# Serving six gathered rows ahead of tile 64, none in the last six tiles, and spreading the products that add up set 0

## The chip, the cores and the metric

The kernel runs on one NeuronCore of a Trainium2 chip. The metric is device time in microseconds of one execution. The engines work at once and meet at semaphores: TensorE (PE, with its weight loads as PEld), VectorE (DVE), ScalarE (ACT), GpSimd (POOL) and SyncE (SP). POOL and SP also issue transfers: SP the plain ones, POOL the indirect ones (gathers by index), and one set of 16 DMA engines carries both.

## The reference, cut to what matters

The model has two layers. Each ends in a feed-forward stage in which every one of 256 tokens picks 16 experts for each of 8 heads out of 16384:

```
u = jnp.take(expert_u, idx, axis=0)
act = gelu(einsum('chkd,cd->chk', u, xc))
vsel = jnp.take(expert_v, idx, axis=0)
return einsum('chk,chkd->cd', gate * act, vsel)
x = x + peer_ffn(rms_norm(x, norm_ffn[l]), ...)
```

An expert is one row of 2048 numbers of `peer_u` and one of `peer_v`. The change lies in this stage alone.

## The kernel before, in words

The stage is the function `experts`, called once in each layer. It treats the 256 tokens in two ways.

160 tokens (`DENSE`) are done densely on PE. **Sweep 1** runs over 128 tiles of `peer_u`; a tile is 128 experts, 1 MB, 16 products of 128x160 (L1753). SP streams the tiles into a ring of four (`ex_tile`). ACT takes each result through the GELU (L1870, L1872). From tile 64 (`FIRST`) to tile 103, each tile is preceded by a product of one-hot matrices that spreads the gates of four tokens over the experts (L1762); ACT copies it (L1909), DVE multiplies it in (L2083) and builds the next one-hot matrices (L1999, L2000). DVE also multiplies each tile's GELU by its gates (L2086). **Sweep 2** runs over 128 tiles of `peer_v` (L1826), which POOL gathers (L1703), by index lists `ex_wanted` that DVE makes eight tiles at a time (`want`, L2012 to L2014: 13 of the 16 pieces in tiles 104 to 116, the last three after the loop over the tiles).

The other 96 tokens come in three sets of 32. A set has 32 picks in each of four partition quarters, so a *row step* gathers one expert row for each of 128 partitions: 32 steps in `peer_u` (a dot product on DVE, L2028), then 32 in `peer_v` (a weighted sum on DVE, L2031 and L2034). That makes 192 steps, numbered n = 0 to 191. Steps 0 to 31 are the dots of set 0, 32 to 63 its sums, 64 to 95 the dots of set 1, and so on. POOL gathers them, 1 MB each, into a ring of three (`ex_row`): the gather of step n waits until step n-3 is served. `served(j)` says how many steps DVE has done by the end of sweep 1's tile j: 30 before tile 64, then one with each tile, 94 at the end. `rows_ahead` derives from it how many gathers POOL issues before sweep 2's first tile (92), each as two half rows (L1692); after that five gathers of whole rows (L1686) are put between every six gathers of `peer_v` tiles, all in one queue, in order. Step 32 needs `weigh(0)` on ACT (L1895), which takes the dots of set 0 through the GELU; the same holds for the other sets.

When a set is summed, four small products (`fold`, L1789) add its quarters up and DVE adds each into `x` (`fold_add`, L2043). They use two PSUM banks in turn, so the third product of a set waits for the first addition. Set 0 is folded in front of tiles 114 to 117 (`FOLD_0`), set 1 in front of tiles 64, 66, 68 and 70 of sweep 2, with DVE's additions in front of steps 147, 149, 151 and 153. `widen` (L1776) spreads a set's tokens over the partitions before its dots.

In front of tile 62 PE transposes the picks (L1801), for which DVE must have made the shares (`share(0)`, L1971 to L1973), for which ACT must have taken the exponentials (`exps(0)`, L1877, in front of tile 60). ACT copies the transposed picks (L1904), and DVE can build one-hot matrices.

Two more waits matter. PE's tile j waits until ACT has taken tile j-3 (three banks). From tile 66 on ACT's GELU of tile j goes into one of two buffers and waits until DVE has multiplied tile j-2.

Each engine runs its own program in the order written, and a wait holds all that stands behind it on that engine, its transfers too.

Of the kernel before, what the change touches and what calls it, by code (L numbers as in the profile page):

```python
# [8 lines left out]
P = 128  # L9
# [7 lines left out]
TB = SEQ // P  # L17
# [13 lines left out]
PEER_H, KEYS, TOPK = 8, 128, 16  # L31
# [5 lines left out]
SET, SETS, STEPS = 32, 3, 32  # L37
# [2 lines left out]
GROUP = 4  # L40
GROUPS = DENSE // GROUP
FIRST = 64
BEFORE = 30
WIDEN_0, EXPS_1, WIDEN_1, FOLD_0 = 2, 16, 90, 114
WIDEN_2, FOLD_1, FOLD_1_AT = 28, 64, 147
A_BANKS = (4, 5, 3)
G_BANKS = (0, 1, 2)
# [1539 lines left out]

def served(j):

    return BEFORE + max(j - FIRST + 1, 0)  # L1590


def experts(nc, t, layer, sem, sb, bank, c, x, hT, query, W, low, layer_base, row_in, v_in, cols, cols_in):
# [22 lines left out]
    with ExitStack() as st:  # L1616
# [19 lines left out]
        share_w = sb(st, "ex_share", [P, SETS, STEPS])  # L1636
        dot, dot_gelu = sb(st, "ex_dot", [P, STEPS]), sb(st, "ex_dot_gelu", [P, STEPS])
        weight = sb(st, "ex_weight", [P, STEPS])

        over = lambda name, shape, kb, dt=F32: nc.alloc_sbuf_tensor_at(name, shape, dt, offset=int(scratch + kb * 1024))  # L1640
        left, cand = over("ex_left", [P, 256], 0), over("ex_cand", [P, TOPK, TOPK], 1)
# [5 lines left out]
        pos = over("ex_pos", [P, TOPK], 5.375, U32)  # L1647
        half_u = over("ex_half_u", [P, 2, TOPK], 5.5, U32)
        half_f = over("ex_half_f", [P, 2, TOPK], 5.625)
        total = over("ex_total", [P, TB, 2, PEER_H], 5.75)  # L1650
        picks = nc.alloc_sbuf_tensor_at("ex_picks", [P, TB, 3, PEER_H, TOPK], F32, offset=before_hot)
        best = nc.alloc_sbuf_tensor_at("ex_best", [P, TB, PEER_H, TOPK], F32, offset=before_hot + 3072)
        outT = W[:, 0:KT, :]
# [3 lines left out]
        with nc.Block() as block:  # L1657
# [59 lines left out]
            def _(pe):  # L1717
# [61 lines left out]
                def fold(s, n):  # L1779

                    pe.wait_ge(sums_ready, s + 1)
                    r = slice(SET * (s + 1), SET * (s + 2))
                    if n >= 2:
                        pe.wait_ge(fold_added, 4 * s + n - 1)
                    elif s < 2:
                        pe.wait_ge(wide_out, (7, 11)[s] + n)
                    else:
                        pe.wait_ge(fold_added, 7 + n)
                    mmul(bank[r, 6 + n % 2, :], c("fold"), sums[:, n * GW:n * GW + GW], start=True, stop=True)\  # L1789
                        .then_inc(fold_mm, 1)  # L1790

                for j in range(TILES):
                    if 0 <= j - WIDEN_0 < 4:
                        widen(0, j - WIDEN_0)
                    if j == FIRST - 2:
                        pe.wait_ge(picks_ready, TB)
                        pe.wait_ge(wide_out, 3)
                        for i in range(3):
                            for b in range(TB):
                                n = min(P, DENSE - b * P)  # L1800
                                mm = tr(bank[:, 6, i * DENSE + b * P:i * DENSE + b * P + n],  # L1801
                                        picks[0:n, b, i].rearrange("p h k -> p (h k)"), c("ident")[0:n, 0:n])
                        mm.then_inc(picks_mm, 1)
                    if 0 <= j - FIRST < GROUPS:
                        gates(j - FIRST)
                    if 0 <= j - WIDEN_1 < 4:
                        widen(1, j - WIDEN_1)
                    if 0 <= j - FOLD_0 < 4:
                        fold(0, j - FOLD_0)
                    tile(j)  # L1810

                pe.wait_ge(gates_times, GROUPS)
# [34 lines left out]
            def _(act):  # L1847
# [49 lines left out]
                for j in range(TILES):  # L1897
                    if j == EXPS_1:
                        exps(1)
                    if j == FIRST - 4:  # L1900
                        exps(0)
                    if j == FIRST - 2:
                        act.wait_ge(picks_mm, 1)
                        A.copy(picksT[:].rearrange("p a s -> p (a s)"), bank[:, 6, 0:3 * DENSE]).then_inc(picks_out, 1)  # L1904
                    g = j - FIRST
                    if 0 <= g < GROUPS:
                        act.wait_ge(gates_mm, g + 1)
                        src = bank[:, G_BANKS[g % len(G_BANKS)], :].rearrange("p (c e) -> p e c", c=GROUP)
                        A.copy(W[:, j:TILES, GROUP * g:GROUP * g + GROUP], src[:, j:TILES, :]).then_inc(gates_put, 1)  # L1909
                    for s, first in enumerate((WIDEN_0, WIDEN_1)):  # L1910
                        if j == first - 1:
                            if s == 0:
                                act.wait_ge(h_scaled, 4)
                            four_times(s, 0)
                        if 0 <= j - first < 4:
                            widened(s, j - first)
                    tile(j)
                    if served(j - 1) < STEPS <= served(j):
                        weigh(0)
                weigh(1)  # L1920
                four_times(2, 0)
                for g in range(4):
# [2 lines left out]
                for i in range(6):  # L1925
                    act.wait_ge(out_mm, i + 1)
                    n = min(3, KT - 3 * i)
# [4 lines left out]
            def _(dve):  # L1932
# [130 lines left out]
                    for n in range(2 * h, 2 * h + 2):  # L2063
                        serve(n)
                over_best(0)
                for n in range(2 * PEER_H, served(FIRST - 1)):
                    serve(n)
                share(0)

                dve.wait_ge(picks_out, 1)  # L2070
                one_hot(0)
                one_hot(1)

                for j in range(FIRST, TILES):
                    g = j - FIRST
                    if 0 <= j - FOLD_0 < 4:
                        fold_add(0, j - FOLD_0)
                    if g < GROUPS:
                        dve.wait_ge(gates_put, g + 1)
                        dve.wait_ge(tile_out, j)  # L2080
# [69 lines left out]
```

## Time and profile before

| | |
|---|---|
| Time before, median of 3 runs | 3850.46 us (3844.37 to 3850.97) |
| The profiled execution | 3844.62 us, span 3842.8 us |
| PE busy | 3703.6 us (96%) |
| DVE busy | 2355.8 us (61%) |
| POOL busy | 1222.3 us (32%) |
| L1753, products of sweep 1 | 8192, 1133.9 us |
| L1826, products of sweep 2 | 8192, 1116.7 us |
| L2028, dots of gathered rows | 192, mean 2292 ns |
| L2034, sums of gathered rows | 186, mean 2350 ns |

Busy time is a share of the span. The span runs from the first to the last instruction. Times in a timeline count from its start. Sweep 1 of layer 1 begins at 2648.83 us, sweep 2 at 3262.55 us; in layer 0 they begin at 733.92 us and 1348.59 us.

### The profile page before, as it was taken

Reading aid. Unit: us, or ns where it says so; the run is one execution under the profiler, and the core shown is the slowest. Engines: PE = TensorE matmul, PEld = TensorE weight load, DVE = VectorE, ACT = ScalarE, POOL = GpSimd, SP = SyncE. Lnnn points to the kernel's source line nnn. Section 1 sums busy time; section 2 is a strip of 40 time slices with the busy share of each in tenths; the row PEclk is TensorE's granted clock in tenths of the full one; section 3 lists DMA queues with packets and bytes.
Section 4 is the critical chain, followed back from the end, with each engine's and each line's share of the span. In section 5 each row is a group of like instructions: output and inputs, shape, how many; then the busy total and the mean of one; then the engine's idle time right before and its main releaser. Section 6 shows DMA issues by size and latency. Waiting matters only on the chain. (4 is left out here: it accounts for less than half of the span.)

```text
span 3842.8 us, 63592 instructions
## 1 busy us (share of the span) xinstructions
PE 3703.6 (96%) x26848; PEld 3413.9 (89%) x26848; DVE 2355.8 (61%) x4207; ACT 429.8 (11%) x1020; POOL 1222.3 (32%) x936
## 2 busy tenths in 40 slices
PE   7998999999999999999979989999999999999998
PEld 6776895899999899999967868959999998999998
DVE  5975853884488754444369658538944986544442
ACT  1013220100111000000010132211101110000000
POOL 2610000033133365655335110000331334555553
PEclk9998999999999999999989989999999999999999
DMA  5441013499899999999644311135998999999996
GB/s 163 132 131 32 29 39 128 168 389 406 327 401 398 378 367 363 366 352 369 246 137 137 121 32 34 57 105 187 400 406 321 402 398 387 377 367 361 352 367 218
DMA packets 312250, 994.19 MB, mean 259 GB/s; under 512 B 59309, under 2 KB 170285, under 8 KB 230509
## 3 DMA queue, kind: packets, MB, share of 16 engines
q0 software_dynamic: 118656, 587.71, 39.5%
q1 hardware_dynamic: 193312, 402.41, 28.8%
q8 instruction: 214, 3.51, 0.4%
q14 instruction: 68, 0.56, 0.0%
HBM read 1071.38 MB, written 2.10 MB: 279 GB/s over the span
## 5 line engine op out<-in xcount | busy, mean ns | idle before, releaser
L1753 PE MATMUL bank<-ycT,ex_tile 128*128 128x160 f32 x8192 | 1133.9, 300 | 0.0
L1753 PEld LDWEIGHTS bank<-ycT,ex_tile 128*128 128x128 f32 x8192 | 1119.2, 190 | 8.7 <-issue 8.4
L1826 PEld LDWEIGHTS bank<-ex_W,ex_tile 128*128 128x128 f32 x8192 | 1113.3, 190 | 8.0 <-issue 6.7
L1826 PE MATMUL bank<-ex_W,ex_tile 128*128 128x160 f32 x8192 | 1116.7, 299 | 1.1 <-DMA ex_tile<-in_peer_v,ex_wanted 1.1
L2028 DVE CUSTOM_DVE_ANT_0 ex_row<-ex_row,ex_h_wide 128x2048 f32<-128x2048 f32 x192 | 439.1, 2292 | 389.1 <-DMA ex_row<-in_peer_u,ex_rows 386.8
L2034 DVE SCALAR_TENSOR_TENSOR ex_sums<-ex_row,ex_weight,ex_sums 128x2048 f32<-128x2048 f32 x186 | 437.1, 2350 | 364.1 <-DMA ex_row<-in_peer_v,ex_rows 364.1
L1692 POOL DMA_INDIRECT ex_row<-in_peer_u,ex_rows x240 | 259.0, 1079 | 1205.1 <-DVE ex_rows L1986 759.5
L1703 POOL DMA_INDIRECT ex_tile<-in_peer_v,ex_wanted x256 | 338.2, 1321 | 428.0 <-PE bank L1826 397.6
L335 PE MATMUL pj_bank<-pj_hT,pj_piece 128*128 128x256 f32 x2048 | 458.0, 383 | 2.5 <-DVE pj_hT L606 2.5
L335 PEld LDWEIGHTS pj_bank<-pj_hT,pj_piece 128*128 128x128 f32 x2048 | 387.4, 191 | 68.3 <-issue 13.8
L1692 POOL DMA_INDIRECT ex_row<-in_peer_v,ex_rows x128 | 121.3, 948 | 311.4 <-DVE ex_sums L2034 168.3
L1686 POOL DMA_INDIRECT ex_row<-in_peer_v,ex_rows x128 | 170.7, 1334 | 46.3 <-issue 41.4
L812 PE MATMUL bank<-arena,ycT 128*128 128x512 f32 x320 | 140.0, 593 | 2.0 <-PEq L904 2.0
L1011 PE MATMUL bank<-arena 128*128 128x128 f32 x1152 | 140.3, 280 | 0.0
L1011 PEld LDWEIGHTS bank<-arena 128*128 128x128 f32 x1152 | 136.6, 195 | 0.9
L812 PEld LDWEIGHTS bank<-arena,ycT 128*128 128x128 f32 x320 | 60.2, 190 | 75.5 <-issue 75.3
L1178 POOL TENSOR_TENSOR ycT<-ycT,rw_H 128x1024 f32<-128x1024 f32 x6 | 15.9, 2646 | 322.2 <-DVE rw_H L1349 321.8
L1467 PE MATMUL bank<-ycT,query_w 128*128 128x256 f32 x512 | 114.9, 382 | 2.0 <-PEq L1484 2.0
L1686 POOL DMA_INDIRECT ex_row<-in_peer_u,ex_rows x72 | 106.9, 1484 | 21.9 <-issue 21.9
L1872 ACT ACTIVATE ex_W<-bank 128x160 f32<-128x160 f32 (+20 forms) x206 | 56.9, 276 | 496.0 <-PE bank L1753 496.0
L1467 PEld LDWEIGHTS bank<-ycT,query_w 128*128 128x128 f32 x512 | 95.8, 190 | 16.5 <-issue 2.7
L2000 DVE TENSOR_SCALAR ex_hot<-consts,ex_picksT 128x128 f32<-128x128 f32 x320 | 110.1, 344 | 0.0
(385 smaller groups left out, 3457.6 us busy)
## 6 DMA issues: line engine op xcount, KB each, us to landing
ex_tile<-in_peer_uT SPq DMA_DIRECT2D x256, 1024.0 KB, 8.1
pj_piece<-in_w_in SPq DMA_DIRECT2D x32, 2048.0 KB, 8.7
arena<-in_w_out SPq DMA_DIRECT2D x20, 1024.0 KB, 5.1
query_w<-in_peer_w_query SPq DMA_DIRECT2D x16, 1024.0 KB, 6.1
rw_low_rank<-in_w_out SPq DMA_DIRECT2D x12, 512.0 KB, 3.5
ex_row<-in_peer_u,ex_rows POOLq DMA_INDIRECT x312, 9.7
ex_row<-in_peer_v,ex_rows POOLq DMA_INDIRECT x256, 8.9
ex_tile<-in_peer_v,ex_wanted POOLq DMA_INDIRECT x256, 8.2
```

The costliest lines, as they stand in the source:

```text
L335: mm = mmul(pj_bank[:, n % 2, m * SEQ:m * SEQ + SEQ], piece[:, n % 2, k, m * P:m * P + P], hT[:, k, :], start=(m == 0 and k == 0), stop=(k ...
L812: mm = nc.tensor.matmul(bank[:, out_bank(n) + b, :], ycT[:, br * GT + k, b * P:b * P + P], out_w["place"][:, i % PLACES, k, :], start=(br ...
L1011: mm = mmul(bank[:, b, j * P:j * P + P], left[:, d, j, :], right[:, d, j, :], start=(j == 0), stop=True, skip_group_check=True)
L1467: mm = nc.tensor.matmul(bank[:, h % 2, 0:SEQ], query["w"][:, h % WRING, k, :], hT[k // 4][:, k % 4, :], start=(k == 0), stop=(k == KT - 1) ...
L1686: nc.gpsimd.indirect_dma_start(out=place[:, n % RING, :], out_offset=None, in_=whole_rows[table][:, :], in_offset=bass.IndirectOffsetOnAxi ...
L1692: nc.gpsimd.indirect_dma_start(out=place[:, n % RING, half * D // 2:(half + 1) * D // 2], out_offset=None, in_=tables[table][:, :], in_off ...
L1703: nc.gpsimd.indirect_dma_start(out=ring[:, slot, :], out_offset=None, in_=whole_rows[1][:, :], in_offset=bass.IndirectOffsetOnAxis(ap=want ...
L1753: mm = mmul(o, ring[:, j % SLOTS, k * P:k * P + P], hT[k // 4][:, k % 4, 0:DENSE], start=(k == 0), stop=(k == KT - 1))
L1826: mm = mmul(bank[:, at_, lo:lo + DENSE], ring[:, i % SLOTS, m * P:m * P + P], W[:, j, :], start=(j == 0 and m % 3 == 0), stop=(j == TILES ...
L2000: mm = V.tensor_scalar(hot1[:, g % 2, i, :], c("iota"), picksT[:, 0, n:n + 1], picksT[:, 2, n:n + 1], ALU.is_equal, ALU.mult)
L2028: V.tensor_tensor_reduce(out=row, in0=row, in1=h_wide[:], scale=1.0, scalar=0.0, op0=ALU.mult, op1=ALU.add, accum_out=dot[:, step:step + 1 ...
L2034: V.scalar_tensor_tensor(sums[:], row, weight[:, step:step + 1], sums[:], ALU.mult, ALU.add)\
```

## The change

`served` now counts 36 steps before tile 64, then one with each tile up to 94: tiles 64 to 121 have one each, tiles 122 to 127 none. Six more steps (30 to 35) so stand on DVE between `over_best(0)` and tile 64: steps 30 and 31 ahead of `share(0)`, 32 to 34 behind it, and 35 behind the first one-hot matrices. ACT's `exps(0)` moves from tile 60 to tile 56, and `weigh(0)` stands in front of tile 59. The gathers that POOL issues ahead of sweep 2 grow from 92 to 96. `widen(1)` moves from tiles 90 to 93 to tiles 78 to 81. The folds of set 0 stand in front of tiles 112, 113, 118 and 119. `total` gets a place of its own, since the sums of set 0 now begin while it is in use.

```diff
-BEFORE = 30
-WIDEN_0, EXPS_1, WIDEN_1, FOLD_0 = 2, 16, 90, 114
+BEFORE, LAST = 36, 58
+WIDEN_0, EXPS_1, EXPS_0, WEIGH_0, WIDEN_1 = 2, 16, FIRST - 8, FIRST - 5, 78
+FOLD_0_AT = (112, 113, 118, 119)
...
-    return BEFORE + max(j - FIRST + 1, 0)
+    return BEFORE + min(max(j - FIRST + 1, 0), LAST)
...
+        total = sb(st, "ex_total", [P, TB, 2, PEER_H])
...
-        total = over("ex_total", [P, TB, 2, PEER_H], 5.75)
...
-                    if 0 <= j - FOLD_0 < 4:
-                        fold(0, j - FOLD_0)
+                    if j in FOLD_0_AT:
+                        fold(0, FOLD_0_AT.index(j))
...
-                    if j == FIRST - 4:
+                    if j == EXPS_0:
                         exps(0)
+                    if j == WEIGH_0:
+                        weigh(0)
...
-                    if served(j - 1) < STEPS <= served(j):
-                        weigh(0)
...
-                for n in range(2 * PEER_H, served(FIRST - 1)):
+                for n in range(2 * PEER_H, STEPS):
                     serve(n)
                 share(0)
-
+                for n in range(STEPS, served(FIRST - 1) - 1):
+                    serve(n)
                 dve.wait_ge(picks_out, 1)
                 one_hot(0)
                 one_hot(1)
+                serve(served(FIRST - 1) - 1)
...
-                    if 0 <= j - FOLD_0 < 4:
-                        fold_add(0, j - FOLD_0)
+                    if j in FOLD_0_AT:
+                        fold_add(0, FOLD_0_AT.index(j))
```

PE, the end of sweep 1, before (16 products of L1753 are one tile, `ex_sums` marks a fold; the first row is tiles 103 to 113):

```order
L1753 MATMUL bank<-ycT,ex_tile 128x160 x176
L1789 MATMUL bank<-ex_sums,consts 32x512
L1753 MATMUL bank<-ycT,ex_tile 128x160 x16
L1789 MATMUL bank<-ex_sums,consts 32x512
L1753 MATMUL bank<-ycT,ex_tile 128x160 x16
L1789 MATMUL bank<-ex_sums,consts 32x512
L1753 MATMUL bank<-ycT,ex_tile 128x160 x16
L1789 MATMUL bank<-ex_sums,consts 32x512
L1753 MATMUL bank<-ycT,ex_tile 128x160 x176
```

And now (every line number behind the constants is one higher):

```order
L1754 MATMUL bank<-ycT,ex_tile 128x160 x144
L1790 MATMUL bank<-ex_sums,consts 32x512
L1754 MATMUL bank<-ycT,ex_tile 128x160 x16
L1790 MATMUL bank<-ex_sums,consts 32x512
L1754 MATMUL bank<-ycT,ex_tile 128x160 x80
L1790 MATMUL bank<-ex_sums,consts 32x512
L1754 MATMUL bank<-ycT,ex_tile 128x160 x16
L1790 MATMUL bank<-ex_sums,consts 32x512
L1754 MATMUL bank<-ycT,ex_tile 128x160 x144
```

The folds start two tiles sooner, and between the second and the third now lie five tiles where there was one.

POOL's queue around the start of sweep 2, before (`ex_row` rows are gathers of steps, `ex_tile` rows those of `peer_v` tiles; x56 is 28 steps in halves, 64 to 91):

```order
L1692 DMA ex_row<-in_peer_u,ex_rows 128x1024 x56
L1703 DMA ex_tile<-in_peer_v,ex_wanted 128x2048 x2
L1686 DMA ex_row<-in_peer_u,ex_rows 128x2048
L1703 DMA ex_tile<-in_peer_v,ex_wanted 128x2048
L1686 DMA ex_row<-in_peer_u,ex_rows 128x2048
L1703 DMA ex_tile<-in_peer_v,ex_wanted 128x2048
L1686 DMA ex_row<-in_peer_u,ex_rows 128x2048
```

And now:

```order
L1693 DMA ex_row<-in_peer_u,ex_rows 128x1024 x64
L1704 DMA ex_tile<-in_peer_v,ex_wanted 128x2048 x2
L1687 DMA ex_row<-in_peer_v,ex_rows 128x2048
L1704 DMA ex_tile<-in_peer_v,ex_wanted 128x2048
L1687 DMA ex_row<-in_peer_v,ex_rows 128x2048
L1704 DMA ex_tile<-in_peer_v,ex_wanted 128x2048
L1687 DMA ex_row<-in_peer_v,ex_rows 128x2048
```

Behind the first two tiles of sweep 2 the queue held step 92, and behind each of the next ones 93 and 94; now it holds 96, 97 and 98 there, four steps further on, and so all through sweep 2.

DVE, the gap in front of tile 64, now (`ex_total` marks `share(0)`, `ex_sums` steps 32 to 34 of set 0; before, the one-hot matrices, L1999 there, stood right behind the third row). The first one-hot row is the last shown:

```order
L1972 TENSOR_REDUCE ex_total<-ex_picks 128x8
L1973 RECIPROCAL ex_total<-ex_total 128x8
L1974 TENSOR_TENSOR ex_picks<-ex_picks,ex_total 128x128
L2024 TENSOR_TENSOR ex_weight<-ex_dot_gelu,ex_share 128x32
L2032 TENSOR_SCALAR ex_sums<-ex_row,ex_weight 128x2048
L2027 REGISTER_ALU
L2035 SCALAR_TENSOR_TENSOR ex_sums<-ex_row,ex_weight,ex_sums 128x2048 x2
L2000 TENSOR_SCALAR ex_hot<-consts,ex_picksT 128x128
```

Three sum steps came in between the shares and the one-hot matrices; the step behind those is not shown.

## Rows read from the trace of the kernel before

**Rows 1.** Chain of waits, layer 1: start, us, engine, line, count.

```profile
2672.51 247.76 PE bank L1753 x1824
...
2935.55 0.89 PE bank L1762 x8
2936.45 4.35 PE bank L1753 x32
...
3131.22 0.30 ACT ex_gelu L1870
```

**Rows 2.** PE timeline, layer 1, end of sweep 1: start, us, idle before and releaser.

```profile
3137.15 47.98 PE L1753 MATMUL bank<-ycT,ex_tile 128*128 128x160 f32 x352
3185.06 1.05 PE L1789 MATMUL bank<-ex_sums,consts 128*32 128x512 f32 x2
...
3191.55 4.61 PE L1753 MATMUL bank<-ycT,ex_tile 128*128 128x160 f32 x32
3205.53 1.88 PE L1789 MATMUL bank<-ex_sums,consts 128*32 128x512 f32 x2 [9.36 <-DVE x L2043]
3207.34 6.22 PE L1753 MATMUL bank<-ycT,ex_tile 128*128 128x160 f32 x32
...
3214.47 48.08 PE L1753 MATMUL bank<-ycT,ex_tile 128*128 128x160 f32 x352
```

**Rows 3.** PE timeline, layer 0: the same fold, and the start of sweep 2.

```profile
1290.34 1.89 PE L1789 MATMUL bank<-ex_sums,consts 128*32 128x512 f32 x2 [9.01 <-DVE x L2043]
...
1348.59 122.02 PE L1826 MATMUL bank<-ex_W,ex_tile 128*128 128x160 f32 x896 [1.07 <-DMA ex_tile<-in_peer_v,ex_wanted]
```

**Rows 4.** DVE timeline, layer 1, tiles 104 to 127 of sweep 1 and after.

```profile
3147.36 2.29 DVE L2028 CUSTOM_DVE_ANT_0 ex_row<-ex_row,ex_h_wide 128x2048 f32<-128x2048 f32 x1 [0.65 <-DMA ex_row<-in_peer_u,ex_rows]
...
3192.03 2.29 DVE L2028 CUSTOM_DVE_ANT_0 ex_row<-ex_row,ex_h_wide 128x2048 f32<-128x2048 f32 x1 [2.58 <-DMA ex_row<-in_peer_u,ex_rows]
...
3196.06 0.32 DVE L2086 TENSOR_TENSOR ex_W<-ex_W,ex_gelu 128x160 f32<-128x160 f32 x1
3196.31 2.29 DVE L2028 CUSTOM_DVE_ANT_0 ex_row<-ex_row,ex_h_wide 128x2048 f32<-128x2048 f32 x1
...
3204.70 0.68 DVE L2043 TENSOR_TENSOR x<-bank,x 32x512 f32<-32x512 f32 x1
3205.41 0.33 DVE L2086 TENSOR_TENSOR ex_W<-ex_W,ex_gelu 128x160 f32<-128x160 f32 x1
...
3256.24 2.29 DVE L2028 CUSTOM_DVE_ANT_0 ex_row<-ex_row,ex_h_wide 128x2048 f32<-128x2048 f32 x1
3258.46 0.08 DVE L2028 DVE_READ_ACCUMULATOR2_ANT ex_dot<- 128x1 f32 x1
...
3272.81 1.48 DVE L2012 TENSOR_REDUCE ex_hot<-ex_W 128x8 f32<-128x1280 f32 x1
...
3278.22 2.29 DVE L2028 CUSTOM_DVE_ANT_0 ex_row<-ex_row,ex_h_wide 128x2048 f32<-128x2048 f32 x1
```

**Rows 5.** Windows: stretch, its length, busy PE, PEld, DVE, ACT, POOL; clock, DMA, GB/s.

```profile
2888.00:2921.00 33.00, 33.00 (x243) 32.60 (x241) 0.78 (x3) 5.31 (x11) 1.86 (x2) 1.00 0.83 319
...
3000.00:3060.00 60.00, 60.00 (x460) 60.00 (x459) 54.81 (x128) 7.42 (x33) 21.64 (x24) 1.00 1.02 401
...
3137.00:3185.00 48.00, 48.00 (x355) 47.88 (x354) 32.22 (x46) 3.28 (x11) 18.00 (x18) 1.00 1.02 414
3185.00:3207.00 22.00, 12.64 (x71) 9.20 (x70) 18.97 (x26) 0.91 (x3) 7.51 (x8) 0.85 1.01 404
```

**Rows 6.** DVE timeline, layer 1, the gap in front of tile 64.

```profile
2885.41 2.29 DVE L2028 CUSTOM_DVE_ANT_0 ex_row<-ex_row,ex_h_wide 128x2048 f32<-128x2048 f32 x1 [2.76 <-DMA ex_row<-in_peer_u,ex_rows]
...
2913.58 0.29 DVE L1971 TENSOR_REDUCE ex_total<-ex_picks 128x8 f32<-128x128 f32 x1 [25.86 <-ACT ex_picks L1877]
...
2922.12 0.29 DVE L1999 TENSOR_SCALAR ex_hot<-consts,ex_picksT 128x128 f32<-128x128 f32 x1 [7.70 <-ACT ex_picksT L1904]
```

**Rows 7.** POOL timeline, layer 1: a half-row gather.

```profile
2889.22 0.94 POOL L1692 DMA_INDIRECT ex_row<-in_peer_v,ex_rows  x1 [0.30 <-issue]
```

**Rows 8.** Tile `ex_tile`, its gathers at 3786:3825 and at 3250:3300.

```profile
DMA to landing us min/median/max: 5.0/5.2/6.5
...
DMA to landing us min/median/max: 7.7/8.7/10.0
```

**Rows 9.** Timelines of PE and DVE, layer 1: first fold of set 1 and its addition.

```profile
3542.42 1.04 PE L1789 MATMUL bank<-ex_sums,consts 128*32 128x512 f32 x2
...
3550.05 0.69 DVE L2043 TENSOR_TENSOR x<-bank,x 32x512 f32<-32x512 f32 x1
```

## The prediction

> **What bounds the kernel now.** I read the chain of waits first, layer 1's feed-forward stage. It is PE almost throughout: sweep 1 runs at 247.76 / 57 = 4.35 us a tile, and at 4.35 + 0.89 = 5.24 us with a gate product [rows 1]. So only places where PE waits, or would now wait, can move the time. The PE timeline then shows one wait in sweep 1: the third fold of set 0 stands 9.36 us (9.01 in layer 0) for DVE's addition of the first [rows 2, 3]. Behind it the engine runs slow: this fold takes 1.88 us where the first took 1.05, and the next tile 6.22 where the one before took 4.61, and in that stretch the granted clock is 0.85, partly at 1.2 GHz [rows 2, 5]. That is 9.36 + 0.83 + 1.61 = 11.8 us, and the second way to count agrees: tiles 104 to 127 free of waits would take 24 x 4.35 + 4 x 0.97 = 108.3 us from 3141.5 (3137.15 + 4.35, tile 103 being the first of the eleven) to 3249.8, and sweep 1 ends at 3214.47 + 48.08 = 3262.55, 12.7 us later.
>
> DVE is late because its rows are. From the step of tile 104 at 3147.36 to that of tile 111 at 3192.03, seven steps take 44.67 us, 6.38 each, all ended by a DMA wait [rows 4], while PE goes at 4.35 and the DMA engines are full at 414 GB/s [rows 5]. The tile stream takes 1.05 MB per 4.35 us = 241 GB/s, and 1.05 MB / (414 - 241) is 6.1 us: rows get what tiles leave.
>
> **The change, part by part.** Worked in layer 1, taken twice.
>
> *The gap.* DVE idles 25.86 us ahead of `share(0)` and 7.70 us behind it, and the DMA engines run at 319 GB/s there [rows 5, 6]. Steps 30 and 31 were already on their way; at one row per 6.4 us they end near 2900. `share(0)` then waits for an exponential four tiles (17.4 us) earlier than 2913.5, and is done near 2901 instead of 2914. Step 32 waits for `weigh(0)` in front of tile 59, near 2908; steps 32 to 34 end near 2919, with row 34 landing last. DVE has to be free at 2922.1 for the one-hot matrices [rows 6]; they take 3.6 us, step 35 ends near 2928, and the gates of tile 64 are multiplied at 2931.7. So the six steps fit with about 3 us to spare, and I cost them at 0. If rows 33 and 34 come later than I think, the price is one row, 6.4 us, less the 3 of slack and the 2.8 that the one-hot matrices can slip: 0 to about 1 us.
>
> *Tiles 64 to 103.* Same steps per tile, 5.24 us a tile and 2.1 MB in it, 401 GB/s used [rows 1, 5]. The ring of rows is full at tile 64 as before. 0. `widen(1)` only moves.
>
> *The folds.* The third now stands at tile 118 and needs the addition of tile 112. DVE reaches tile 112 at 3196.06 [rows 4], PE reaches tile 118 near 3205. The wait goes, 12.7 us with its clock.
>
> *What is late next.* PE's tile j+5 waits for ACT's tile j+2, which waits for DVE's multiplication of tile j: 0.33 + 0.30 us [rows 1, 4] and small change, so tile j+5 cannot start before T(j) + 0.7. Now DVE: T(112) = 3196.06 + 0.7 for its addition (3204.70 to 3205.41) = 3196.8. Row, `want` piece and multiplication take about 4.3 us when the row is there, one more 0.85 with an addition; the ring holds the row of tile 112 at 3196.31, the next land each 6.3 us. That gives T(113) = 3202.2, T(114) = 3206.8, T(115) = 3213.1, T(116) = 3219.5. PE unheld starts tile 121 at 3141.5 + 17 x 4.35 + 3.9 = 3219.4, and DVE allows 3220.2. From here DVE's rows hold PE. Six more rows follow (tiles 116 to 121). Held, PE takes tiles no faster than rows come, so both share: 2.1 MB at 401 GB/s is 5.2 us. T(122) = 3219.5 + 31.2 = 3250.7, tile 127 starts at 3251.4, and sweep 1 ends at 3255.8: 6.8 us gained. When the last `peer_u` tile is in, rows come faster: before, the two at 3256.24 and 3258.77 stand 2.5 us apart [rows 4]. So I take 3254.1, a gain of 8.5. The ends: 12.7 if rows keep up, 0 if they stay at 6.38 a step to the end (T(122) = 3257.8, end 3262.9).
>
> *The start of sweep 2.* POOL's queue is in order. Gather 97 stands ahead of `peer_v` tile 3 and waits for step 94. Step 94 lies behind the loop over tiles and three `want` pieces: with E the start of sweep 2, ACT's GELU (0.30) and the multiplication (0.33) of tile 127 end near E + 0.95, three pieces (3272.81 to 3278.22, 5.41) bring E + 6.4, the step takes 2.3 more, and gather 97 goes at E + 8.9, tile 3 at E + 10.1 (0.94 + 0.30) [rows 4, 7]. Before, the gather at this place was step 93, whose condition (step 90) was met before E. A tile lands 5.2 us after its issue when alone, 8.7 under load [rows 8]; with one row ahead of it I take 6, E + 16.1. PE wants it at E + 13.05. Stall 3.0 us; ends 2.1 (5.0) and 5.8 (8.7) with 1.6 to 2.4 more if the clock falls. The trace has an idle of 1.07 us at this place in layer 0 after which 28 tiles take 122 us, so no fall [rows 3], and one of 9.36 with a fall; 3 us lies between, nearer the first: 0.
>
> The Trainium skill (DMA: Bandwidth & Descriptors, "Anatomy of one DMA — SWDGE (gpsimd) path") puts a transfer at 2.0 us fixed plus its bytes at 436 GB/s, by which 1.05 MB lands in an estimated 4.4 us, under the 5.0 us of the fastest tile here. By that figure the stall would be 1.5 us and the total 3 us better; the trace's landing is longer and decides.
>
> *The middle of sweep 2.* All steps run four further on, 4.8 tiles or 21 us earlier. The first fold of set 1 ended at 3543.4 and DVE came to its addition at 3550.05 [rows 9]; now DVE is there 14 us early and waits. Gather 150, which needs step 147 (3543.4 + 0.7 + 2.3, then 0.3), goes at about 3547 and holds `peer_v` tile 66, issued at 3548.2. PE wants tile 66 at 3553.3. With 6 us to land: 3554.2, stall 0.9; ends 0 and 3.6. The later additions find slack of two tiles and more.
>
> *The end of sweep 2* waits for no step. 0.
>
> Sum per layer: -8.5 + 3.0 + 0.9 = -4.6; both -9.2. The profiled execution's own 3844.62 becomes 3835.4. The median shown is 5.8 above it, and two of three runs lie there, so for the median I say 3850.46 - 9.2 = 3841.3.
>
> **The rivals.** All against the median.
>
> *Full gain:* rows keep up, because rows saved from the gap's idle transfers leave the ring fuller and the lag of 15 us at tile 112 stops growing. -2 x (12.7 - 3.9) = -17.6, and -25.4 if the waits in sweep 2 do not bite either: 3825 to 3833. For it: the allowance is nearly five tiles, and only six tiles come after it is used up. Against: 6.38 us a row over seven rows, with no sign of recovery while PE runs.
>
> *No net change, the transfers bound it:* rows stay near 6.3 a step until sweep 1 ends, the tail gains 0 to 3, the two new waits cost 3.9: 2 x (3.9 - 1.5) = +4.8, 3855. For it: 414 GB/s in that stretch is the highest in the windows. The bytes that PE and DVE need are the same.
>
> *Slower, POOL's queue:* the wait in front of `peer_v` tile 3 is the loaded one, 5.8 us, and the clock falls behind it, 2.4 more, and tile 66 costs 3.6: 11.8 a layer against the 8.5. Then +6.6 in all with the tail as forecast and +10 with a tail of 6.8: 3857 to 3861. It decides from the point where a gather behind the row lands in over 7.5 us. For it: 8.7 is the median under load. Against: at E + 8.9 nothing else is in flight.
>
> *The gap holds PE:* a late row 34 puts the one-hot matrices behind PE at tile 64 in both layers. The change then doesn't do what it says at no cost: some +3 each on top of the forecast, 3847, or worse.
>
> **How the numbers follow.** Forecast 0.45 (own range 3833 to 3847), full gain 0.22, no net change 0.14, slower queue 0.13, gap 0.06. A measurement of this kernel can tell 0.2%, 7.7 us, from no change. Faster by more: the full gain 0.22 and some 0.6 of the forecast's 0.45: 0.50. Slower by more: 0.11 of the queue, 0.03 of the others: 0.14. The same: 0.36. The range, with under 2 in 10 left out, is 3826 to 3857.
>
> **What would show it.** The idle in front of the third fold gone, PE held in its place by ACT's GELU in front of tiles 121 to 127, with T(112) near E(112) + 15; DVE's additions at tiles 112 and 113. In the gap no PE idle, `share(0)` near 2901. At sweep 2's tile 3 an idle of some 3 us ended by a DMA, ahead of it POOL waiting for DVE's step 94; at tile 66 one of about 1. The prediction is wrong if sweep 1 loses more than 8 us to DVE's rows, or if POOL's waits reach PE with more than 6 us per layer.

## The result and the profile after

The changed kernel takes 3854.18 us, median of 20 runs (3851.46 to 3862.57), the kernel before 3847.59 us, median of 20 (3844.17 to 3852.08): ratio 1.0018, interval 1.0011 to 1.0025. I had said 3841.3, faster; it is slower. The profiled execution took 3862.57 us (span 3860.8), the slowest of the 20 and 8.4 above their median, so stages are read in it and totals are compared by medians.

The PE timeline of the changed kernel, layer 1, answers to [rows 2] (start, length, idle before and releaser; 32 records of L1754 or L1827 are one tile, two for each of its 16 products):

```profile
3146.81 39.28 PE L1754 MATMUL bank<-ycT,ex_tile 128*128 128x160 f32 x288
...
3214.45 1.04 PE L1790 MATMUL bank<-ex_sums,consts 128*32 128x512 f32 x2
3219.97 1.04 PE L1790 MATMUL bank<-ex_sums,consts 128*32 128x512 f32 x2
3220.95 30.69 PE L1754 MATMUL bank<-ycT,ex_tile 128*128 128x160 f32 x224
3254.14 10.61 PE L1754 MATMUL bank<-ycT,ex_tile 128*128 128x160 f32 x64 [2.50 <-ACT ex_gelu L1871]
3266.23 13.31 PE L1827 MATMUL bank<-ex_W,ex_tile 128*128 128x160 f32 x96 [1.48 <-DMA ex_tile<-in_peer_v,ex_wanted]
3283.15 17.09 PE L1827 MATMUL bank<-ex_W,ex_tile 128*128 128x160 f32 x104 [3.61 <-DMA ex_tile<-in_peer_v,ex_wanted]
...
3553.00 1.05 PE L1790 MATMUL bank<-ex_sums,consts 128*32 128x512 f32 x2
3553.98 8.96 PE L1827 MATMUL bank<-ex_W,ex_tile 128*128 128x160 f32 x64
3568.01 1.92 PE L1790 MATMUL bank<-ex_sums,consts 128*32 128x512 f32 x2 [5.07 <-DMA ex_tile<-in_peer_v,ex_wanted]
3569.86 9.99 PE L1827 MATMUL bank<-ex_W,ex_tile 128*128 128x160 f32 x64
3579.77 1.04 PE L1790 MATMUL bank<-ex_sums,consts 128*32 128x512 f32 x2
...
3843.25 3.81 PE L1790 MATMUL bank<-ex_sums,consts 128*32 128x512 f32 x8
```

The third fold has no idle left (before, 9.36 us). From the start of tile 103 to the start of sweep 2 (E = 3266.23 - 1.48 = 3264.75) it is now 117.9 us, before 125.2 (the first row of sweep 2 starts at 3262.39 there; 3262.55 is the modelled end of the row ahead of it); layer 0 gives 117.2 against 125.2. From E to the last folds it is 578.5 us where it was 562.9 (3825.30 - 3262.39), in layer 0 578.55 against 564.1. So the stages gain 7.3 us in layer 1 and 8.0 in layer 0, and lose 15.6 and 14.4: 14.7 us more in all. The medians are only 6.6 us apart; part of the difference is that sweep 1's end is slower in this execution than in others (see "Why the prediction was wrong"). In sweep 2 PE waits at three places. Layer 0 has the same three:

```profile
1343.10 13.31 PE L1827 MATMUL bank<-ex_W,ex_tile 128*128 128x160 f32 x96 [0.51 <-DMA ex_tile<-in_peer_v,ex_wanted]
1361.93 111.39 PE L1827 MATMUL bank<-ex_W,ex_tile 128*128 128x160 f32 x800 [5.52 <-DMA ex_tile<-in_peer_v,ex_wanted]
...
1646.03 1.92 PE L1790 MATMUL bank<-ex_sums,consts 128*32 128x512 f32 x2 [4.61 <-DMA ex_tile<-in_peer_v,ex_wanted]
```

The windows of the changed kernel (columns as in [rows 5]): the gap now moves 415 GB/s instead of 319 (408 in the window shifted by the 9.7 us that this execution is later there), PE is busy throughout it, and behind the wait at tile 3 the granted clock is 0.66, partly at 1.2 GHz, where the kernel before has 1.00 in the same 10 us.

```profile
2888.00:2921.00 33.00, 33.00 (x245) 33.00 (x244) 12.22 (x14) 5.11 (x11) 9.25 (x9) 1.00 1.02 415
...
3280.00:3290.00 10.00, 6.85 (x30) 6.85 (x31) 4.70 (x2) 0.00 (x0) 8.01 (x5) 0.66 0.99 378
```

POOL's timeline at these places, `ex_row` being gathers of steps and `ex_tile` those of `peer_v` tiles:

```profile
3253.64 3.05 POOL L1693 DMA_INDIRECT ex_row<-in_peer_u,ex_rows  x1 [5.10 <-DVE ex_dot L2029]
3256.99 0.94 POOL L1693 DMA_INDIRECT ex_row<-in_peer_u,ex_rows  x1 [0.30 <-issue]
3258.23 1.00 POOL L1704 DMA_INDIRECT ex_tile<-in_peer_v,ex_wanted  x1 [0.31 <-issue]
...
3273.35 2.76 POOL L1687 DMA_INDIRECT ex_row<-in_peer_v,ex_rows  x1 [10.13 <-DVE ex_dot L2029]
3276.41 1.69 POOL L1704 DMA_INDIRECT ex_tile<-in_peer_v,ex_wanted  x1 [0.30 <-issue]
...
3557.38 2.76 POOL L1687 DMA_INDIRECT ex_row<-in_peer_u,ex_rows  x1 [11.22 <-DVE ex_dot L2029]
3560.44 0.99 POOL L1704 DMA_INDIRECT ex_tile<-in_peer_v,ex_wanted  x1 [0.30 <-issue]
```

And DVE's at the same times (the last line is the first addition of set 1):

```profile
3265.13 0.33 DVE L2089 TENSOR_TENSOR ex_W<-ex_W,ex_gelu 128x160 f32<-128x160 f32 x1 [4.02 <-ACT ex_gelu L1871]
3265.37 1.48 DVE L2013 TENSOR_REDUCE ex_hot<-ex_W 128x8 f32<-128x1280 f32 x1
...
3270.79 2.29 DVE L2029 CUSTOM_DVE_ANT_0 ex_row<-ex_row,ex_h_wide 128x2048 f32<-128x2048 f32 x1
3273.00 0.09 DVE L2029 DVE_READ_ACCUMULATOR2_ANT ex_dot<- 128x1 f32 x1
3273.00 2.29 DVE L2029 CUSTOM_DVE_ANT_0 ex_row<-ex_row,ex_h_wide 128x2048 f32<-128x2048 f32 x1
...
3554.09 0.69 DVE L2044 TENSOR_TENSOR x<-bank,x 32x512 f32<-32x512 f32 x1 [14.26 <-PE bank L1790]
```

Gather 97 waits 10.13 us for step 94, which stands behind the three `want` pieces. It is then issued 0.35 us into DVE's step 95, and takes 2.76 us where a gather beside an idle DVE took 0.94 [rows 7]. Tile 3, behind it, is issued at E + 11.66 and used at E + 18.4. The same happens at gather 150 and tile 66: DVE waits 14.26 us for PE's first fold of set 1, so step 147 is late, and with it the gather that waits for it.

### The profile page after: what moved, and what is told of

Its sections match the earlier page's. It is cut to its first block and busy times, and to the rows that moved or that the text cites. A ratio compares the mean times of both kernels' runs of the same rounds, so it can differ in the third digit from the quotient of the medians.

```text
span 3860.8 us, 63482 instructions
## 1 busy us (share of the span) xinstructions
PE 3710.6 (96%) x26848; PEld 3418.7 (89%) x26848; DVE 2356.8 (61%) x4207; ACT 429.3 (11%) x1020; POOL 1206.5 (31%) x944
## 5 line engine op out<-in xcount | busy, mean ns | idle before, releaser
L1827 PEld LDWEIGHTS bank<-ex_W,ex_tile 128*128 128x128 f32 x8192 | 1120.7, 191 | 20.8 <-DMA ex_tile<-in_peer_v,ex_wanted 12.4
L1754 PE MATMUL bank<-ycT,ex_tile 128*128 128x160 f32 x8192 | 1133.2, 299 | 5.5 <-ACT ex_gelu L1871 5.5
L1827 PE MATMUL bank<-ex_W,ex_tile 128*128 128x160 f32 x8192 | 1125.0, 300 | 11.2 <-DMA ex_tile<-in_peer_v,ex_wanted 11.1
L1754 PEld LDWEIGHTS bank<-ycT,ex_tile 128*128 128x128 f32 x8192 | 1117.6, 190 | 13.4 <-issue 13.0
L2035 DVE SCALAR_TENSOR_TENSOR ex_sums<-ex_row,ex_weight,ex_sums 128x2048 f32<-128x2048 f32 x186 | 437.1, 2350 | 368.5 <-DMA ex_row<-in_peer_v,ex_rows 362.3
L2029 DVE CUSTOM_DVE_ANT_0 ex_row<-ex_row,ex_h_wide 128x2048 f32<-128x2048 f32 x192 | 438.8, 2292 | 327.1 <-DMA ex_row<-in_peer_u,ex_rows 312.1
L1704 POOL DMA_INDIRECT ex_tile<-in_peer_v,ex_wanted x256 | 327.1, 1278 | 429.0 <-PE bank L1827 393.0
L1693 POOL DMA_INDIRECT ex_row<-in_peer_v,ex_rows x128 | 125.2, 978 | 250.8 <-DVE ex_sums L2035 188.7
L2044 DVE TENSOR_TENSOR x<-bank,x 32x512 f32<-32x512 f32 x24 | 16.6, 690 | 187.2 <-PE bank L1790 187.0
```

The costliest lines, as they stand in the source:

```text
L1693: nc.gpsimd.indirect_dma_start(out=place[:, n % RING, half * D // 2:(half + 1) * D // 2], out_offset=None, in_=tables[table][:, :], in_off ...
L1704: nc.gpsimd.indirect_dma_start(out=ring[:, slot, :], out_offset=None, in_=whole_rows[1][:, :], in_offset=bass.IndirectOffsetOnAxis(ap=want ...
L1754: mm = mmul(o, ring[:, j % SLOTS, k * P:k * P + P], hT[k // 4][:, k % 4, 0:DENSE], start=(k == 0), stop=(k == KT - 1))
L1827: mm = mmul(bank[:, at_, lo:lo + DENSE], ring[:, i % SLOTS, m * P:m * P + P], W[:, j, :], start=(j == 0 and m % 3 == 0), stop=(j == TILES ...
L2029: V.tensor_tensor_reduce(out=row, in0=row, in1=h_wide[:], scale=1.0, scalar=0.0, op0=ALU.mult, op1=ALU.add, accum_out=dot[:, step:step + 1 ...
L2035: V.scalar_tensor_tensor(sums[:], row, weight[:, step:step + 1], sums[:], ALU.mult, ALU.add)\
```

## The experiments

All but the first were timed in five rounds beside the kernel before, whose median was 3847.48, 3846.29 or 3847.78 us in these sets of rounds. The ratio compares the runs and can differ from the quotient of the medians by 0.0006. "Ahead" counts the gathers that POOL issues before `peer_v` tile 0.

| Kernel | Median, us | Ratio to before | Interval |
|---|---|---|---|
| the change | 3854.18 | 1.0018 | 1.0011 to 1.0025 |
| steps 94, 95 before `want` | 3847.38 | 0.9994 | 0.9985 to 1.0003 |
| additions of set 1 at 151 | 3839.50 | 0.9976 | 0.9967 to 0.9985 |
| both of these | 3832.53 | 0.9955 | 0.9942 to 0.9968 |
| folds alone (92 ahead) | 3849.87 | 1.0005 | 0.9997 to 1.0014 |
| step 94 alone before `want` | 3848.55 | 1.0007 | 0.9998 to 1.0016 |
| 94 ahead, additions at 149 | 3824.73 | 0.9942 | 0.9928 to 0.9955 |
| 94 ahead, additions at 149, steps 94, 95 before `want` | 3824.84 | 0.9943 | 0.9929 to 0.9956 |
| folds alone, 88 ahead | 3851.20 | 1.0014 | 1.0005 to 1.0023 |
| gap alone (96 ahead) | 3875.63 | 1.0072 | 1.0059 to 1.0086 |
| folds alone, 90 ahead | 3841.42 | 0.9987 | 0.9978 to 0.9996 |
| gap alone, 94 ahead | 3846.59 | 0.9996 | 0.9987 to 1.0005 |
| 95 ahead, additions at 148 | 3827.90 | 0.9953 | 0.9939 to 0.9966 |

**Are the two places in POOL's queue the cause?** First the wait at tile 3 alone, by serving its steps sooner:

```diff
+                for n in range(served(TILES - 1), 3 * STEPS):
+                    serve(n)
                 for i in range((FIRST + GROUPS) // CHUNK, TILES // CHUNK):
                     want(i)
```

> The changed kernel with steps 94 and 95 put ahead of the three want pieces behind the loop over tiles; nothing else. Queue theory (the loss sits in POOL's queue, gather 97 behind step 94): step 94 ends near E + 3.2 instead of E + 8.3 (E is where sweep 2 starts), peer_v tile 3 is issued near E + 6.6 and lands near E + 13.3, when PE wants it; the idle of 3.6 and 5.5 us at tile 3 and the 3 us of slow clock behind it go, the idle at tile 66 stays: some 15 us less than the changed kernel's 3854, 3839, ratio to before 0.998. Rival (transfers: the same bytes in a full stretch, order does not matter): the idle turns up at another tile of the first ten, time within 3 us of 3854, ratio 1.001 to 1.002.

Then the wait at tile 66 alone, `FOLD_1_AT` 147 to 151, and both together.

> The changed kernel with DVE's four additions of set 1 in front of steps 151, 153, 155, 157 instead of 147 to 153; nothing else. Queue theory: DVE comes to the first addition when PE's fold is done, gather 150 is not held, the idle of 4.6 to 5.1 us at peer_v tile 66 and 2 us of slow clock behind it go, tile 3 stays: some 13 us less than 3854, 3841, ratio to before 0.998. Rival (transfers): the idle moves to a tile nearby, time within 3 us of 3854.

> Both edits of the two kernels before on the changed kernel. Queue theory: what is left is the gain in sweep 1, 7.5 to 8 us a layer against before, less an idle of 0.5 to 1.5 us at the start of sweep 2: ratio to before 0.994 to 0.996, 3825 to 3833. Rival (transfers): under 5 us better than the changed kernel, ratio 1.000 or above.

The second and the third came out as the queue says. In the second PE passes the set 1 folds without a wait (3535, 3545, 3555, 3565 us in its PE timeline, each 9.87 after the last), and 14.7 us of the changed kernel's time are gone. The first took 6.8 us off the change, where the queue said 15. Its PE timeline, in the rows below, shows a part of the reason: the wait at tile 3 is gone and no clock fall follows, but 1.43 us stand in front of tile 0 and 1.06 in front of tile 6 (0.46, 1.43 and 0.27 at tiles 0, 5 and 6 in layer 0). From E to the last folds it is 5.6 us (layer 1) and 4.9 (layer 0) shorter than in the changed kernel, 10.5 together; why the medians show only 6.8 is open.

```profile
3260.48 26.51 PE L1827 MATMUL bank<-ex_W,ex_tile 128*128 128x160 f32 x192 [1.43 <-DMA ex_tile<-in_peer_v,ex_wanted]
3288.05 12.22 PE L1827 MATMUL bank<-ex_W,ex_tile 128*128 128x160 f32 x88 [1.06 <-DMA ex_tile<-in_peer_v,ex_wanted]
```

**Which part brings the gain?** The kernel before with only the folds moved:

```diff
-WIDEN_0, EXPS_1, WIDEN_1, FOLD_0 = 2, 16, 90, 114
+WIDEN_0, EXPS_1, WIDEN_1 = 2, 16, 90
+FOLD_0_AT = (112, 113, 118, 119)
```

> The kernel before with its set 0 folds in front of tiles 112, 113, 118, 119 and nothing else of the change. If the folds alone carry the gain in sweep 1: the 9 us idle at the third fold gone, PE held a little by ACT's GELU from tile 121 on, 7 to 8 us a layer, ratio to before 0.996. If the rows served in the gap are what makes it possible (fewer rows at the end): PE is held by DVE's rows up to tile 127 and gains under 3 us a layer, ratio 0.999 to 1.000.

The idle at the third fold went with the folds alone, and the time did not, for a reason that neither expectation had. It stood at the start of sweep 2 instead, 9.03 us in layer 0 and 11.00 in layer 1. This is PE, and POOL in the same kernel:

```profile
3264.83 25.38 PE L1827 MATMUL bank<-ex_W,ex_tile 128*128 128x160 f32 x165 [11.00 <-DMA ex_tile<-in_peer_v,ex_wanted]
```

```profile
3248.23 3.01 POOL L1693 DMA_INDIRECT ex_row<-in_peer_u,ex_rows  x1 [1.66 <-DVE ex_dot L2029]
3251.55 2.31 POOL L1693 DMA_INDIRECT ex_row<-in_peer_u,ex_rows  x1 [0.30 <-issue]
...
3256.64 1.00 POOL L1704 DMA_INDIRECT ex_tile<-in_peer_v,ex_wanted  x1 [0.31 <-issue]
```

The 92 gathers stand ahead of `peer_v` tile 0, and the last of them wait for steps that DVE serves late. Tile 0 is issued 2.8 us after sweep 1 has ended (3253.83). Then the gap part alone, the changed kernel with `FOLD_0_AT = (114, 115, 116, 117)`:

> The changed kernel with the products and additions of set 0 where the kernel before has them (tiles 114 to 117): the gap part of the change alone, with its 96 gathers ahead of sweep 2. Theory A (the two parts are separate: the gap does not shorten the wait at the third product, and the waits at peer_v's tiles 3 and 66 belong to the gap part): the 9.0 and 9.4 us of idle at the third product come back, and the idles at tiles 0, 3 and 66 of sweep 2 stay: 3860 to 3872 us, 1.004 to 1.0065 of the kernel before. Rival (the later fold makes VectorE's additions, and so step 94, late; with the old places the waits of sweep 2 are shorter or gone): idle at tiles 3 and 66 under 2 us, 3845 to 3852 us, 0.999 to 1.001.

10.74 and 8.39 us stand at the third fold again, and sweep 2 has all its waits: at tile 3, 5.50 and 6.12 us, at tile 66, 4.86 and 5.41. The end of sweep 1, from tile 103 to sweep 2, is as long as before (125.9 and 124.6 us). So the folds brought the whole gain of sweep 1, and the gap part with its 96 gathers ahead brought the waits at tiles 3 and 66, though not without use: the 9 and 11 us that the folds alone have in front of tile 0 are 0.51 and 1.48 with it. My sum for this kernel was 4 us short: 3847.8 + 14.4 + 15.6 would have given 3878.

**Why the gather's issue takes 2.76 us.** Step 94 ahead of `want`, step 95 behind it, so that gather 97 is issued beside `want`'s reductions:

```diff
+                serve(served(TILES - 1))
                 for i in range((FIRST + GROUPS) // CHUNK, TILES // CHUNK):
                     want(i)
-                for n in range(served(TILES - 1), ROWS_IN):
+                for n in range(served(TILES - 1) + 1, ROWS_IN):
```

> The changed kernel, with one of its two late steps (94) served ahead of the three pieces of ex_want and the other (95) behind them. Theory A (a gather's issue takes 2.76 us instead of 0.94 only where VectorE works on a row of 2048 columns at the same time): gather 97 is issued beside the pieces of ex_want, takes 0.9 to 1.0 us, and tile 3's idle of 3.6 to 5.5 us is under 0.5 us; at the most 1 us of it turns up at tile 4, the clock does not fall at the start of sweep 2, and tile 66 keeps its 4.6 to 5.1 us: about 3844 us, 0.997 to 0.999 of the kernel before. Theory B (the long issue belongs to the step that POOL has waited for, whatever VectorE does next): gather 97 takes 2.76 us again, and 1.5 to 2 us of idle stay at tiles 3 and 4.

POOL, then DVE, of this kernel:

```profile
3253.75 0.95 POOL L1687 DMA_INDIRECT ex_row<-in_peer_v,ex_rows  x1 [4.21 <-DVE ex_dot L2029]
3255.00 0.99 POOL L1704 DMA_INDIRECT ex_tile<-in_peer_v,ex_wanted  x1 [0.30 <-issue]
3261.37 1.80 POOL L1687 DMA_INDIRECT ex_row<-in_peer_v,ex_rows  x1 [5.38 <-DVE ex_dot L2029]
3263.48 2.89 POOL L1704 DMA_INDIRECT ex_tile<-in_peer_v,ex_wanted  x1 [0.30 <-issue]
```

```profile
3253.40 1.48 DVE L2013 TENSOR_REDUCE ex_hot<-ex_W 128x8 f32<-128x1280 f32 x1
...
3263.16 2.35 DVE L2035 SCALAR_TENSOR_TENSOR ex_sums<-ex_row,ex_weight,ex_sums 128x2048 f32<-128x2048 f32 x1
```

Gather 97 has waited for its step as before, and takes 0.95 us beside a reduction. Tile 4's gather has waited for nothing and takes 2.89 beside a row operation. So Theory A holds for the issue. The total does not: the wait moved to tile 4 and was 2.5 to 2.7 us, because gather 98 now waits for step 95 behind `want`. I had allowed it 1 us, and the time is 3848.55 where I had said about 3844.

**Does the count ahead decide?** The changed kernel with two gathers fewer ahead and the additions of set 1 moved along:

```diff
-WIDEN_2, FOLD_1, FOLD_1_AT = 28, 64, 147
+WIDEN_2, FOLD_1, FOLD_1_AT = 28, 64, 149
...
-    return min(served(TILES - SLOTS - 1) + RING - 1 + j * 5 // 6, ROWS_IN)
+    return min(served(TILES - SLOTS - 1) + RING - 3 + j * 5 // 6, ROWS_IN)
```

> The changed kernel, with 94 gathers ahead of sweep 2 instead of 96, every later one two steps later in the same rhythm, and the additions of set 1 two tiles later (147 to 149 as the first). Theory A (the time lost in sweep 2 is POOL's queue: a gather that waits for a VectorE step stands in front of the peer_v transfer that TensorE needs): the idles at tiles 0, 3 and 66 all go, both layers together give some 14 us against the kernel before: 3829 to 3834 us, 0.995 to 0.9965. Rival (the rows then come too late for VectorE in sweep 2, whose steps wait for their gathers): the idles of TensorE go, but VectorE ends sweep 2 later and the time is 3845 us or more, 0.999 or above.

> Both: 94 gathers ahead as in the kernel with two fewer, and the two late steps 94 and 95 served ahead of the pieces of ex_want. Theory A (with two fewer gathers nothing in POOL's queue waits for these steps any more when peer_v's first tiles are issued): no difference from the kernel with two fewer, within 2 us, 0.995 to 0.9965. Rival (ex_want then ends 4.6 us later and the first products of sweep 2, which read it, begin late): 2 to 8 us slower than that kernel, with an idle of TensorE in front of tile 0.

> The kernel with 94 gathers ahead, with 95 instead, and the additions of set 1 at 148. Theory A (what counts is which peer_v tile stands behind the gather that waits for step 94: now it is one or two tiles later than with 96, and TensorE needs it 4.4 to 9 us later): idles in front of tiles 0 to 5 under 3 us in all in each layer, none at tile 66, 3824 to 3831 us, 0.994 to 0.996. Rival (the margin was two gathers wide and one does not do): over 3 us of idle in one place and a lower clock behind it, 3834 us or more, 0.9965 or above.

The first of these came out below the 3829 to 3834 that I had expected. With 94 ahead PE has no wait from the start of sweep 2 to its end, in either layer:

```profile
3235.22 8.94 PE L1754 MATMUL bank<-ycT,ex_tile 128*128 128x160 f32 x64 [0.32 <-ACT ex_gelu L1871]
3244.00 56.26 PE L1827 MATMUL bank<-ex_W,ex_tile 128*128 128x160 f32 x413
...
3806.91 3.80 PE L1790 MATMUL bank<-ex_sums,consts 128*32 128x512 f32 x8
```

Sweep 2 is back at 562.9 us, and the tail of sweep 1 takes 115.0 and 114.0 us, from the first product of tile 103 to the first of sweep 2, where the kernel before takes 125.2 in both layers: 21.4 less together. The 1.07 us in front of sweep 2 in layer 0 are gone as well. The median is 21.56 below that of the kernel before on the same chip (3846.29). POOL's queue shows that gather 97 is as slow as ever, only now `peer_v` tile 5 stands behind it and not tile 3 (two gathers fewer ahead put each gather two tiles later). Tile 5 is issued at E + 12.1 (E = 3244.00), and PE comes to it five tiles of 4.35 us after E, at E + 21.8:

```profile
3253.00 2.76 POOL L1687 DMA_INDIRECT ex_row<-in_peer_v,ex_rows  x1 [2.71 <-PE bank L1827]
3256.07 1.70 POOL L1704 DMA_INDIRECT ex_tile<-in_peer_v,ex_wanted  x1 [0.30 <-issue]
```

(The view names PE as what ended gather 97's wait; it needs step 94, which DVE ended at 3252.73.) Serving steps 94 and 95 sooner adds nothing any more. With 95 ahead tile 4 stands behind gather 97, and 1.39 and 1.34 us stand in front of it and less at the next: with 94 the margin is less than one tile of 4.35 us. The best time of the study is that with 94.

**Are both parts needed?** The kernel before with the folds moved, and fewer ahead (`RING - 5`, 88, and `RING - 3`, 90; set 1's additions at 143 and 145), and the gap alone with 94:

> The kernel before, with the later products and additions of set 0 (tiles 112, 113, 118, 119) and nothing else of the change, and 88 gathers ahead of sweep 2 instead of 92, the additions of set 1 at 143 to keep their place. Theory A (what undid the move of the products alone, 9 and 11 us of idle in front of tile 0, is one gather too many in front of peer_v's first transfer, and the six rows in the gap are needed for nothing else): the idle in front of tile 0 is under 1 us in both layers, sweep 1 keeps its gain of about 8 us each: 3829 to 3836 us, 0.995 to 0.997. Rival (VectorE has too much to serve without the six rows in the gap, and the lag comes out at the start of sweep 2 as a wait for ex_want or at its first steps): over 5 us of idle stay in front of tile 0 or 1, 0.999 or above.

> The kernel before with the moved products and additions of set 0 alone and 90 gathers ahead of sweep 2, between the 92 (9 and 11 us of idle in front of tile 0, held by POOL's queue) and the 88 (13 and 12 us there, held by rows that come late to VectorE, and by its steps that stand in front of the last values for ScalarE). Theory A (without the six rows of the gap VectorE has one row in each tile up to the last, so that the row and the peer_v tile want the same place in POOL's queue, and there is no good count): over 3 us of idle in front of tile 0 in both layers, 0.997 to 1.001. Rival (there is a count that serves both, and the gap part is not needed): under 2 us of idle there, 0.9945 to 0.997.

> The kernel with 94 gathers ahead, with the products and additions of set 0 back at tiles 114 to 117: the gap part alone with its queue mended. Theory A (the idle of 9 us at the third product comes from the wait for VectorE's addition, which lags TensorE by some 15 us, and the gap does not change it): that idle is there again, none at tiles 0, 3 and 66: 3840 to 3848 us, 0.998 to 1.0005. Rival (with the rows served ahead VectorE's lag at tile 114 is gone): under 4 us of idle at the third product, 0.9945 to 0.9965.

With 88 ahead I had expected an idle under 1 us at best. The wait at the start of sweep 2 was longer than with 92, and of another kind, 13.10 us in layer 0 and 12.12 in layer 1:

```profile
3268.36 6.87 PE L1827 MATMUL bank<-ex_W,ex_tile 128*128 128x160 f32 x37 [12.12 <-ACT ex_gelu L1871]
```

PE waits for ACT, ACT for DVE's multiplications, and these stand in DVE's queue behind rows that are now gathered too late. DVE in the same kernel (3.65 and 2.84 us of such waits follow):

```profile
3253.80 2.29 DVE L2029 CUSTOM_DVE_ANT_0 ex_row<-ex_row,ex_h_wide 128x2048 f32<-128x2048 f32 x1 [5.38 <-DMA ex_row<-in_peer_u,ex_rows]
3256.02 0.08 DVE L2029 DVE_READ_ACCUMULATOR2_ANT ex_dot<- 128x1 f32 x1
3256.02 0.32 DVE L2087 TENSOR_TENSOR ex_W<-ex_W,ex_gelu 128x160 f32<-128x160 f32 x1
```

With 90 ahead both kinds stand there, 1.33 us for `peer_v` and 6.07 for ACT in layer 0, 1.37 and 6.41 in layer 1 (read in an execution 7.4 us above that kernel's median). So without the six rows of the gap the folds' move was worth 6.4 us at best (3847.78 - 3841.42) among three counts; other counts were not tried. The gap alone, with 94 ahead, has 9.99 and 9.96 us at the third fold, nothing in sweep 2, and the time of the kernel before. The two parts together, with 94 ahead, are worth 21.6.

## Why the prediction was wrong

*The third fold and sweep 1's tail:* said -8.5 a layer, measured -8.0 and -7.3 in the profiled execution. There PE is held by ACT's GELU as forecast: 1.64, 0.88 and 0.46 us at the end of sweep 1 in layer 0, 2.50 in layer 1. But that is the slowest execution of the 20, and the agreement is in part luck. Four of the kernels keep everything ahead of sweep 2 as it is in the changed one (steps 94, 95 or 94 alone before `want`, additions at 151, and both of these), so their profiles show the same tail again. With the changed kernel's own that makes ten layers: the tail takes 113.4 to 117.9 us against 125.2, a gain of 7.3 to 11.9, 10.1 in the mean, and in five of the ten PE is not held at all. In the kernel with the additions at 151, layer 1, it runs from the last fold to the end of sweep 1 without a wait:

```profile
3206.79 39.39 PE L1754 MATMUL bank<-ycT,ex_tile 128*128 128x160 f32 x288
3247.14 13.31 PE L1827 MATMUL bank<-ex_W,ex_tile 128*128 128x160 f32 x96 [0.97 <-DMA ex_tile<-in_peer_v,ex_wanted]
```

So the hold by DVE's rows is weaker than I had it, and the 10.2 and 11.2 us of the kernel with 94 ahead lie in the same spread. Why executions differ there is open.

*The gap:* said 0 and was. PE has no wait there. `share(0)` came at 2908.89 and the sixth step ended at 2937.7. This execution is 9.66 us later by then than that of the kernel before (tile 103 at 3146.81 against 3137.15), so on the clock of the prediction these are 2899.2 and 2928.0, where it says 2901 and 2928. The rival that the gap holds PE fell.

*The start of sweep 2:* the step that failed. The mechanism was the one written down, and gather 97 went at E + 8.6 (said: 8.9). From there on every size was low. Its issue took 2.76 us and not 0.94, so tile 3 was issued at E + 11.66 instead of 10.1. It was used 6.74 us later instead of 6. Together 5.3 us late instead of 3.0, of which 1.48 stand in front of tile 0 and 3.61 in front of tile 3. That tile 0 would wait I had not said: gather 95, the last ahead of it, waits 5.10 us for DVE, and the first of its two halves takes 3.05. Then the clock. I priced its fall at 0, since an idle of 1.07 us had brought none. After 3.61 us it fell, and 104 records took 17.09 us where they take 104 x 143.60 / 1056 = 14.1 (a later row of the same timeline has 1056 in 143.60 us): 2.9 us more, in layer 0 2.6 (800 records, 111.39 against 108.8). Said 3.0, measured 8.0 in layer 1 (1.48 + 3.61 + 2.9) and 8.6 in layer 0.

*Tile 66:* said 0.9, measured 5.07 and 4.61 idle, and 1.9 more for the fold and the two tiles behind it (1.92 + 9.99 against 1.05 + 8.96). Gather 150 went 4.4 us after the first fold's start (said: 4.6). The issue cost 1.8 more again, the landing 7.5 instead of 6, and PE wanted the tile 1 us sooner than I had it.

So the terms 3.0 and 0.9, 3.9 a layer, should have been some 15 (8.0 + 5.07 + 1.9 and 8.6 + 4.61 + 1.9). That is the step that made a forecast of -9.2 into +6.6: the queue cost far more than the sum had, and a tail that gained over 8.5 us in eight of the ten layers above hid a part of it. That the time lies inside the stated range, and within 1 us of the 3855 of the rival "no net change", is luck: that rival had the tail gain 0 to 3 us and the waits cost 3.9. By its order of events the rival "slower, POOL's queue" is what happened. It named the right place and even a clock fall, and its 11.8 us was still too small: it too had the issue at 0.94 and no wait at tile 0. It had the landing too long instead, 8.7 us where 6.74 and 7.5 passed. I gave it 0.13. The bound of the issue was taken from one row in a stretch where DVE was idle, and the trace of the kernel before had shown the other case. POOL and DVE there, in sweep 1:

```profile
3137.47 2.79 POOL L1692 DMA_INDIRECT ex_row<-in_peer_u,ex_rows  x1 [0.30 <-issue]
```

```profile
3137.16 2.29 DVE L2028 CUSTOM_DVE_ANT_0 ex_row<-ex_row,ex_h_wide 128x2048 f32<-128x2048 f32 x1
```

## What to carry to other kernels

When one queue carries both prefetches and gathers that wait for a consumer, ask of each wait which transfer stands next behind it and when that one is needed: here two gathers fewer ahead, with DVE's additions moved along, decided between +0.2% and -0.6%, with the same work and the same order on PE. A part that shows no gain alone may be half of one, so after removing a wait look at the next place where the same lag can come out, and move the queue along with it. Read a stage in more than one execution before you call a term right. Take an issue's duration from rows where the engine beside it does what it will do at the new place; here a gather that VectorE's row step released was issued into the next one.

## What the runs showed of the hardware

In layer 1 of the changed kernel (2660 to 3800 us) POOL issued 86 gathers while DVE was at an operation on a row of 2048 columns (L2029, L2032, L2035). 83 of them ended 0.81 to 0.90 us after that operation ended, and took up to 3.09 us. The other three began within 0.1 us of its start and took 0.95 at most. 309 gathers issued beside no such operation took 1.10 us or less, and 14 beside a TENSOR_REDUCE took 0.94. The kernel before shows the same in 87 of 95; the other eight began in the first or last 0.1 us of the operation and took 1.0 at most. The Trainium skill (SBUF — State Buffer, "SBUF: two separate sides") says that DVE and GpSimd share one pair of ports as an exclusive lock: an operation of DVE takes it in a 2-port mode, or with two SBUF inputs, but the latter only against a GpSimd operation that reads SBUF. That GpSimd cannot write a DMA's descriptors meanwhile, it says of the 2-port mode. The trace fits such a lock: L2029 and L2035 read two rows and hold the issue, the reduction reads one tile and does not. That L2032, which reads one row, held its two as well (both ended 0.86 us after it) would need the 2-port mode, and no run here shows which mode it ran in.

TensorE's granted clock stayed at 1.00 in 10 us that hold a wait of 2.69 or 1.43 us at the start of sweep 2 (one step before `want`, both steps before `want`). It was 0.66 in the 10 us from 3280 behind the wait of 3.61, and 0.50 in the 10 us from 3260 around the one of 11.00. The length of the wait does not decide it alone: in the kernel with both edits one of 1.86 us was followed by 0.87, and 150 records took 22.32 us where they take 20.4; in the changed kernel the 64 records behind the wait of 2.50 took 10.61 where the same 64 took 8.94 in the kernel with 94 ahead. The wait of 3.61 cost 2.9 us more in this way.
